# A hybrid decoder layer on Trainium2: the order of rotary, value and first-head projection groups ahead of the attention

## The reference, cut to what matters

```python
c_q = _rmsnorm(m_cq, mla_q_norm_g[l])                      # (S, 384)
q = (c_q @ mla_w_uq[l]).reshape(B, S, 8, 128 + 64)
q_nope = q[..., :128]
q_rope = _rope(q[..., 128:], cos_h, sin_h)                 # rotary part, 8 heads x 64
c_kv = _rmsnorm(m_ckv, mla_kv_norm_g[l])                   # (S, 256)
kv = (c_kv @ mla_w_ukv[l]).reshape(B, S, 8, 128 + 128)
k_nope, v = kv[..., :128], kv[..., 128:]
y_mla = _mla_attention(q_nope, q_rope, k_nope, k_rope, v) @ w_mla_o[l]
mixed = (sigmoid(gate_a) * y_gla + sigmoid(gate_b) * y_mla) @ w_out[l]
```

## Time and profile before

| | us |
|---|---|
| median of three runs | 1763.31 |
| the profiled execution, whole | 1768.03 |
| its span in the profile | 1766.3 |
| PE busy | 1732.2 (98%) |
| DVE busy | 1035.1 (59%) |
| ACT busy | 769.3 (44%) |
| POOL busy | 846.8 (48%) |

### The profile page before, as it was taken

The page is one execution under the profiler, slowest core; times in us unless marked ns, Lnnn a source line. Parts: engine busy times, 40 slices in busy tenths (PEclk is TensorE's granted clock), DMA queues, the critical chain, the costliest instruction groups (busy, mean ns, idle before and its releaser), DMA issues.

```text
span 1766.3 us, 23560 instructions
## 1 busy us (share of the span) xinstructions
PE 1732.2 (98%) x8432; PEld 1452.6 (82%) x8432; DVE 1035.1 (59%) x1772; ACT 769.3 (44%) x1432; POOL 846.8 (48%) x714
## 2 busy tenths in 40 slices
PE   8999999999999999999999999999999999999998
PEld 7788888888998877788888888778888888888886
DVE  6312411156666377455565635587677676788798
ACT  6534433343554213555553103654444544444442
POOL 6888776551112353232333356688777777400000
PEclk9999999999999999999999999999999999999999
DMA  5433433271452287532443452443335442595333
GB/s 168 142 107 110 124 107 119 71 215 59 100 125 92 83 265 251 149 96 70 132 132 102 167 190 72 167 140 123 114 121 159 149 145 95 181 334 189 96 96 119
DMA packets 234110, 241.78 MB, mean 137 GB/s; under 512 B 39196, under 2 KB 162252, under 8 KB 233996
## 3 DMA queue, kind: packets, MB, share of 16 engines
q1 hardware_dynamic: 196076, 171.85, 31.6%
q10 hardware_dynamic: 37920, 68.43, 11.6%
HBM read 164.47 MB, written 75.77 MB: 136 GB/s over the span
## 4 chain that ended last, share of the span: by engine, by line
PE 83%; DVE 7%; DMA 4%; ACT 2%; issue 2%; POOL 2%; SPq 1%; ACTq 0%; DVEq 0%; POOLq 0%
PE psum_all L1231 23%; PE psum_all L1233 23%; PE psum_all L1232 23%; PE psum_all L1563 2%; DMA ga_st<-d_sga 1%; PE psum_all L1579 1%; PE psum_all L1581 1%; PE psum_all L1580 1%; PE psum_all L1293 1%; PE psum_all L1551 1%; PE psum_all L1549 1%; PE psum_all L1550 1%; PE psum_all L1552 1%; PE psum_all L1297 1%; PE psum_all L1548 1%
## 5 line engine op out<-in xcount | busy, mean ns | idle before, releaser
L1109 POOL CAST w_hi<-w_raw 128x512 fp32r<-128x512 f32 (+3 forms) x78 | 58.3, 748 | 259.4 <-PE psum_all L1233 254.7
L1231 PE MATMUL psum_all<-xT_hi,w_hi 128*128 128x512 f32 x376 | 148.9, 396 | 5.6 <-POOL w_lo L1040 3.1
L1233 PE MATMUL psum_all<-xT_hi,w_lo 128*128 128x512 f32 x376 | 147.0, 391 | 0.0
L1232 PE MATMUL psum_all<-xT_lo,w_hi 128*128 128x512 f32 x376 | 146.9, 391 | 0.0
L1878 DVE TENSOR_TENSOR xp<-psum_all,xp 128x512 f32<-128x512 f32 x18 | 12.4, 690 | 216.6 <-PE psum_all L1233 216.6
L1231 PE MATMUL psum_all<-t_hi,w_hi 128*128 128x512 f32 x352 | 137.4, 390 | 1.2 <-DVE r L2322 0.4
L1233 PE MATMUL psum_all<-t_hi,w_lo 128*128 128x512 f32 x352 | 137.0, 389 | 0.0
L1232 PE MATMUL psum_all<-t_lo,w_hi 128*128 128x512 f32 x352 | 137.0, 389 | 0.0
L1171 POOL TENSOR_TENSOR w_lo<-w_raw,w_hi 128x512 fp32r<-128x512 f32 x88 | 115.2, 1316 | 42.1 <-ACT w_hi L3120 41.9
L1111 POOL TENSOR_TENSOR w_lo<-w_raw,w_hi 128x512 fp32r<-128x512 f32 (+3 forms) x78 | 126.7, 1624 | 6.4
L1125 POOL TENSOR_SCALAR p_sb<-p_sb,small 128x128 f32<-128x128 f32 (+3 forms) x64 | 47.8, 747 | 163.4 <-DVE small L2177 163.4
(11 more groups left out here) (562 smaller groups left out, 5099.6 us busy)
## 6 DMA issues: line engine op xcount, KB each, us to landing
w_raw<-in_w_up_dram SPq DMA_DIRECT2D x44, 512.0 KB, 4.9
fa_raw<-d_f SPq DMA_DIRECT2D x76, 256.0 KB, 2.7
w_raw<-in_w_in_dram SPq DMA_DIRECT2D x36, 512.0 KB, 4.4
d_f<-up_g SPq DMA_DIRECT2D x44, 256.0 KB, 3.3
d_f<-f_sum SPq DMA_DIRECT2D x33, 256.0 KB, 2.9
wd<-in_w_down_dram SPq DMA_DIRECT2D x33, 256.0 KB, 4.5
w_raw<-in_w_out_dram SPq DMA_DIRECT2D x8, 1024.0 KB, 5.3
x_tok<-in_x_dram SPq DMA_DIRECT2D x8, 512.0 KB, 6.3
```

The lines of the kernel that those rows point to most:

```text
L1109: wc.done(nc.gpsimd.tensor_copy(w_hi[b][:, w], src[:, w]))
L1231: pe.matmul(out_ap, ah, bh, start=start and i == 0, stop=False, skip_group_check=more)
L1232: pe.matmul(out_ap, ah, bl, start=False, stop=False, skip_group_check=more)
L1233: last = pe.matmul(out_ap, al, bh, start=False, stop=stop and i == len(terms) - 1, skip_group_check=more)
```

## The change

Four rotary groups go ahead of the values instead of three, with a fourth buffer `qr_hl`. Head 0's projections are put into the last two rounds: query halves behind the values of round 6, key halves behind those of round 7, with the last transposes behind them. ACT's wait for the last GLA stores (`m_out`) moves from behind the loop to its round 6. POOL splits `mla0` before `rope_low(5)` instead of before `rope_low(7)`. Three of the five `c_low` move forward among the `go` groups. In head 0's attention steps the second projection for head 1 goes from step 1 to step 2.

```diff
-        qr_hl = [... for i, at in enumerate((16, 44, 20))]
+        qr_hl = [... for i, at in enumerate((16, 44, 20, 32))]
+        LEAD = 4
...
+        def p0_at(t):
+            return {TT - 2: (0, 1), TT - 1: (2, 3)}.get(t, ())
...
         FILL = {0: 0, 1: 1, 4: 2, 5: 3}
+        FILL0 = {0: 0, 2: 1, 4: 2, 5: 3}
 
         def fill(h, qb):
-            return h + 1 < MH and qb in FILL
+            return h + 1 < MH and qb in (FILL if h else FILL0)
...
             for t in range(TT):                      # POOL
-                if t == TT - 1:
+                if t == 5:
                     split_part(mla0, 0, 1)
                 rope_low(t)
...
             pe.wait_ge(sm["c_low"], QKT)             # PE
-            for t in range(3):
+            for t in range(LEAD):
                 rope_group(t)
             pe.wait_ge(sm["c_low"], QKT + KVT)
-            for t in range(TT + 2):
-                if t < TT:
-                    ...                              # va(t, 0), va(t, 1)
-                else:
-                    for j in (2 * (t - TT), 2 * (t - TT) + 1):
-                        free(("p0", j))
-                        split3(bank(("p0", j)), project_terms(0, j)).then_inc(mm, 1)
-                if t + 3 < TT:
-                    rope_group(t + 3)
+            for t in range(TT):
+                ...                                  # va(t, 0), va(t, 1)
+                for j in p0_at(t):
+                    free(("p0", j))
+                    split3(bank(("p0", j)), project_terms(0, j)).then_inc(mm, 1)
+                if t + LEAD < TT:
+                    rope_group(t + LEAD)
                 if t < TT:
                     pe.wait_ge(sm["rot_ok"], t + 1)
                     for g in range(2):
-                        transposes(("qrT", t, g), [qr_hl[t % 3][:, 4 * g + i, :] for i in range(4)])
+                        transposes(("qrT", t, g), [qr_hl[t % 4][:, 4 * g + i, :] for i in range(4)])
...
             pe.wait_ge(*ev_at[gid[("p0", 3)]])
+            pe.wait_ge(*ev_at[gid[("va", TT - 1, 1)]])
...
+            C_LOW = (7, 8, 10, 11)                   # DVE
-                if i in (7, 9, 11, 13):
-                    c_low((i - 7) // 2)
+                if i in C_LOW:
+                    c_low(C_LOW.index(i))
...
-                if t >= 3:
-                    ve.wait_ge(mm, gid[("qrT", t - 3, 1)] + 1)
-                V.tensor_copy(qr_hl[t % 3][:, :, 0:ROPE].bitcast(F32R), R_[:, :, :]).then_inc(sm["qr_hi"], 1)
+                if t >= 4:
+                    ve.wait_ge(mm, gid[("qrT", t - 4, 1)] + 1)
+                V.tensor_copy(qr_hl[t % 4][:, :, 0:ROPE].bitcast(F32R), R_[:, :, :]).then_inc(sm["qr_hi"], 1)
...
+                if t == TT - 2:                      # ACT
+                    ac.wait_ge(m_out[0], 16 * 8)
+                    ac.wait_ge(m_out[1], 16 * 8)
+                for j in p0_at(t):
+                    A.copy((qT, kT)[j // 2][0][0][:, j % 2 * HALF:(j % 2 + 1) * HALF], got(("p0", j))).then_inc(sm["p0_hi"], 1)
...
-            ac.wait_ge(m_out[0], 16 * 8)
-            ac.wait_ge(m_out[1], 16 * 8)
```

More of the change, by code:

```diff
@@ L567, in block_kernel, with part_of @@
         FILL = {0: 0, 1: 1, 4: 2, 5: 3}
+        FILL0 = {0: 0, 2: 1, 4: 2, 5: 3}
         def fill(h, qb):
-            return h + 1 < MH and qb in FILL
+            return h + 1 < MH and qb in (FILL if h else FILL0)
+        def part_of(h, qb):
+            return (FILL if h else FILL0)[qb]
         ld2_buf = wbuf(slot_no[("mlao", 1)])
@@ L1509, in _ @@
             pe.wait_ge(sm["c_low"], QKT)
-            for t in range(3):
+            for t in range(LEAD):
                 rope_group(t)
             pe.wait_ge(sm["c_low"], QKT + KVT)
-            for t in range(TT + 2):
-                if t < TT:
-                    n = need(("vall", 0))
-                    for q2 in range(2):
-                        free(("va", t, q2))
-                        split3(bank(("va", t, q2)),
-                               [(c_hi[QKT + k][:, t * P:(t + 1) * P], c_lo[QKT + k][:, t * P:(t + 1) * P],
-                                 w_part(n, k, q2 * HALF, HALF), w_part(n, k, q2 * HALF, HALF, True)) for k in range(KVT)]).then_inc(mm, 1)
-                else:
-                    for j in (2 * (t - TT), 2 * (t - TT) + 1):
-                        free(("p0", j))
-                        split3(bank(("p0", j)), project_terms(0, j)).then_inc(mm, 1)
-                if t + 3 < TT:
-                    rope_group(t + 3)
+            for t in range(TT):
+                n = need(("vall", 0))
+                for q2 in range(2):
+                    free(("va", t, q2))
+                    split3(bank(("va", t, q2)),
+                           [(c_hi[QKT + k][:, t * P:(t + 1) * P], c_lo[QKT + k][:, t * P:(t + 1) * P],
+                             w_part(n, k, q2 * HALF, HALF), w_part(n, k, q2 * HALF, HALF, True)) for k in range(KVT)]).then_inc(mm, 1)
+                for j in p0_at(t):
+                    free(("p0", j))
+                    split3(bank(("p0", j)), project_terms(0, j)).then_inc(mm, 1)
+                if t + LEAD < TT:
+                    rope_group(t + LEAD)
                 if t < TT:
@@ L2972, in pj_high @@
                 A.copy((qT, kT)[j // 2][h % 2][0][:, j % 2 * HALF:(j % 2 + 1) * HALF], psum[7]).then_inc(sm["pj_hi"], 1)
-            for t in range(TT + 2):
-                if t < TT:
-                    for q2 in range(2):
-                        g = 2 * t + q2
-                        if g >= 3:
-                            ac.wait_ge(v_out[g % 3], 32 * (g // 3))
-                        A.copy(v_st[g % 3][0][:, :], got(("va", t, q2))).then_inc(sm["va_hi"], 1)
-                else:
-                    for j in (2 * (t - TT), 2 * (t - TT) + 1):
-                        A.copy((qT, kT)[j // 2][0][0][:, j % 2 * HALF:(j % 2 + 1) * HALF], got(("p0", j))).then_inc(sm["p0_hi"], 1)
+            for t in range(TT):
+                for q2 in range(2):
+                    g = 2 * t + q2
+                    if g >= 3:
+                        ac.wait_ge(v_out[g % 3], 32 * (g // 3))
+                    A.copy(v_st[g % 3][0][:, :], got(("va", t, q2))).then_inc(sm["va_hi"], 1)
+                if t == TT - 2:
+                    ac.wait_ge(m_out[0], 16 * 8)
+                    ac.wait_ge(m_out[1], 16 * 8)
+                for j in p0_at(t):
+                    A.copy((qT, kT)[j // 2][0][0][:, j % 2 * HALF:(j % 2 + 1) * HALF], got(("p0", j))).then_inc(sm["p0_hi"], 1)
                 if t < TT:
```

56 lines of the change are left out of this document (26 added, 30 removed).

## The result

The changed kernel takes 1769.95 us (median of 7, 1768.4 to 1770.27) against 1764.85 us for the kernel before on the same chip (median of 7, 1761.69 to 1766.78); the ratio on record is 1.0022 [1.0013, 1.0031], which is 3.9 us, and the two medians by themselves lie 5.1 us apart. Forecast were +3.2 us and 1766.5 us within 1762.0 to 1771.0.

A forecast was written before the change was run, and what follows sets the result against it. PE bounds the kernel, busy 1732.2 of 1766.3 us, with 6.8 us of waits in reach. Waits saved and moved end at a late `mla2` load, +3.2 us at `probs_t(2)`: 1763.3 + 3.2 = 1766.5 us, range 1762.0 to 1771.0.

The forecast's parts named there:

- the gate: Third normalisation stands behind POOL's wait for the `mla2` load, landing at 728.2; PE starts `probs_t(2)` at 729.8, 3.2 us later.
- DVE's first turn at 664.0: First rotary turn on DVE, before at 664.66, comes 0.7 us earlier as POOL's split ends earlier (bounds 0 and 0.84).
- DVE binds: Value rounds 1 and 2: four turns delay bank reads, PE waits 1 to 2 us at three places, 0.7 us late.
- The wait behind `rope_turn(7)`: Second value group of round 5: PE waits 0.8 us for that turn's bank (bounds 0 and 1.2).
- Scores at +1.2: Entry into the attention: first scores start at 715.1, 1.2 us later than before, with 1.1 us idle instead of 1.4.
- Both waits behind them: Between first scores and `probs_t(2)`: waits of 0.92 and 0.39 us vanish, leaving 11.2 us instead of 12.67.
- the first term: End of the value rounds: the last value part ends on DVE at 711.9, 3.4 us later than before.
- The profiled execution: Whole kernel: the profiled execution, 1768.03 us before, would become 1771.2 by the same accounts.
- Rival A: Load of `mla2` lands later than about 728.5 as stores and `d_qr` bunch: +5 us, 1768.3; chance 0.25.
- B: At `probs_t(2)`: stores land fast, the load isn't last, PE goes on at 726.3: -0.3 us, 1763.0; chance 0.13.
- C: Value rounds: DVE keeps up and most of the 6.8 us of waits goes: -5 us, 1758.3; chance 0.10.
- D: Last latent part still ends at 663.4, PE idles 0.6 us there: 1767.2; chance 0.52 together with the main forecast.

The follow-up runs named there:

- f4: Changed kernel with head 0's projections, and ACT's wait for the last GLA stores, put back behind the loop: ratio to before 1.0021 [1.0012, 1.0030].
- e3: Changed kernel with three rotary groups ahead of the values instead of four: ratio to before 1.0017 [1.0007, 1.0026].
- e7: Changed kernel with three rotary groups ahead and SP's load of `mla2` issued before the wait for the value stores: ratio to before 0.9999 [0.9990, 1.0008].
- e1: Changed kernel with POOL's quarters of `mla2` in head 0 behind the normalisations of steps 3 to 6, not 1 to 4: ratio to before 1.0021 [1.0012, 1.0030].
- e4: Kernel before with POOL's quarters of `mla2` in head 0 behind the normalisations of steps 3 to 6, not 1 to 4: ratio to before 1.0020 [1.0010, 1.0029].
- f1: Changed kernel with early `mla2` load, three rotary groups ahead and POOL's split of the value weights in four: ratio to before 0.9994 [0.9985, 1.0003].
- f2: Kernel before with early `mla2` load and POOL's split of the value weights in four: ratio to before 1.0006 [0.9997, 1.0016].
- e2: Changed kernel with 12 unused matmuls on PE in front of the third transposes: ratio to before 1.0019 [1.0009, 1.0029].
- e5: Changed kernel with SP's load of `mla2` issued behind the last value store, before the wait for the stores: ratio to before 1.0005 [0.9997, 1.0014].
- f3: Kernel before with only head 0's projections moved behind the last two value groups, and the buffer that goes with it: ratio to before 0.9998 [0.9989, 1.0007].

## Why the prediction was right, and where it wasn't

The sum held: +3.2 forecast, +3.9 measured, +3.8 in the traces. The mechanism held in its main step, the gate; that the sum came so near owes something to luck, as the last two steps show. By its steps, in old count:

- DVE's first turn at 664.0: measured 663.8 (660.85). The latent part was done at 662.6, forecast 662.75: it ended 1.1 us behind POOL's end as before, and POOL took 4.60 us, as forecast, in place of 5.43.

```profile
654.12 5.48 DVE L2103 SCALAR_TENSOR_TENSOR c_lo<-c_raw,lat_g,c_hi 128x1024 fp32r<-128x1024 f32 x1
```

```profile
653.92 4.60 POOL L1117 TENSOR_TENSOR w_lo<-w_raw,w_hi 128x2048 fp32r<-128x2048 f32 x1
```

- DVE binds: the first value of round 2 at 680.25, measured 680.05, with waits of 1.63, 1.79 and 0.83 us at the three places where 1 to 2 each were named. Right, the third a little under.
- The wait behind `rope_turn(7)`: mechanism right (DVE stood idle 2.56 us for POOL's `qr_hl` ahead of that turn), size 0.24 us, not 0.8.
- Scores at +1.2: +0.7, for that smaller wait. Both waits behind them gone: right.
- **The gate.** Last value part 711.9, measured 711.4; stores landed 4.6 us behind it, measured 3.95 (708.41 to 712.36); load landed 11.7 us behind that, measured 11.84. So `probs_t(2)` was 2.15 us late, not 3.2. From the scores to there PE needed 11.2 us besides the wait, as forecast. The number of the first term was right and its reason was not enough: I had the value part late because PE has two projections ahead of the last value group. f4 has none there and ends it later still; e3 and e7, with the projections and three groups, have it 1.5 to 1.8 us late, and the fourth turn on DVE adds 1.3 to 1.4. How the parts add up in a DMA queue that is full or nearly so (shares of 0.91 and 1.02 from 690 to 710 us) stays open.
- **What no step had:** the clock. The idle time that I worked out as the whole cost costs 1.6 us more behind it. 3.2 less the 1.1 us by which the gate was set too late (729.8 against 728.7), and 1.6 for the clock, is 3.7: two errors of the sum cancel for the greater part, and that is luck.
- The profiled execution: 1771.2 forecast, 1768.92 measured. The forecast was built on an execution that had lost 3.1 us at half clock in a stretch ahead of the stage; the changed kernel's had not.

Rival A didn't come about: its sign was a load that lands later than 728.5, and it landed at 727.2, with a wait of ACT's last copy of 0.91 us in place of 3.13. B and C are excluded by the 2.94 us wait. D is excluded by the absence of a wait on `c_lo`.

## What to carry to other kernels

Work put ahead on the bound engine helps only if the engine that evicts it has time to spare: price a moved group on every engine it touches. When a load stands in a queue behind a wait for stores, follow it to the instruction that needs it, for the saved waits let the bound engine come there sooner as well. Where an instruction that waits for a load stands in front of one that feeds PE, issuing the load earlier took the loss away here; moving the waiting instruction back cost as much at the next place that needs it. Taking one part of a change at a time can name the wrong part when parts meet in one queue: compare all that share it. When a change adds an idle stretch of PE of a few us, look at the granted clock behind it before the sum is closed.

## What the runs showed of the hardware

**One idle stretch, two clocks.** Waits of 2.32 us (e1 and e4), 2.74 (f1), 2.80 (e3), 2.94 (changed) and 3.88 (f2) were followed by the granted clock of 0.50. The wait of 2.57 us before and that of 2.77 in f4 were followed by 1.00. The sharpest case is the wait of 2.44 us near 423 us, in instructions that are the same in every kernel here: 0.50 followed it in before, f4 and e2, 1.00 in the other ten traces that were read. Length alone doesn't decide it, nor do the instructions; what does is open. Where it fell the step behind it took 9.8 to 11.4 us in place of 6.8, so this stretch too moves a whole execution by 3 us and more, whatever the kernel.

**A coin between DVE and POOL.** The last latent part took 4.27 to 5.48 us when DVE began it behind the start of POOL's 2048-column subtraction (before, changed, e1, e5, e7, f4), 1.28 to 1.89 when it began ahead of that (e2, e3, e4, f3), in kernels of either kind. In e4, the kernel before but for POOL's quarters, DVE was 0.6 us ahead:

```profile
653.07 1.64 DVE L2099 SCALAR_TENSOR_TENSOR c_lo<-c_raw,lat_g,c_hi 128x1024 fp32r<-128x1024 f32 x1
```

```profile
653.70 5.43 POOL L1111 TENSOR_TENSOR w_lo<-w_raw,w_hi 128x2048 fp32r<-128x2048 f32 x1
```

and its stage was 75.0 us, 3.1 less than in the profile that the prediction was made from. I take this coin, with the clock near 423 us, for one cause of the spread of a kernel's runs (1761.38 to 1768.63 over 35 runs of the kernel before on one chip); that was not tried. It isn't the only one: the kernels with the split in four, whose latent part stayed short, spread by 5.2 to 6.4 us. Whether a kernel's edits change how often either falls badly is not known, and the ratios would contain it. The 2.6 us wait that the change was to hide is one side of that coin; on the other (e3, e4, f3) PE waits 1.5 to 1.6 us at the same place for POOL's split of the value weights. POOL pays there: its subtraction took 5.43 to 5.48 us where DVE began first, and 4.59 to 4.61 where DVE's last latent part alone met it and began second (changed, e1, e5, e7, f4). Before it took 5.43 too: there DVE's fourth latent part (655.01, 2.87 us) had begun ahead of it. The Trainium skill, page "SBUF — State Buffer", section "Who interferes with whom", states the rule for the blocked side, that the loser waits for the whole of the other's operation; the rows agree for the one that begins second, and the split in four pieces, with which no latent part took over 1.68 us, agrees too.
